# Gate products of a gated linear recurrence in three rounded parts instead of one full-precision product

## The chip, the cores and the metric

One core of one Trainium2 chip runs the whole program. The metric is the device time of one execution in microseconds (us). A core has a matrix engine (TensorE, PE in the profile; its weight loads are PEld), three elementwise engines (VectorE or DVE, ScalarE or ACT, GpSimd or POOL), and SyncE (SP), which issues the transfers from memory. Each engine works through its own instructions in order and waits on semaphores for the others.

## The reference, cut to what matters

Two transformer layers over 256 image tokens and 256 context tokens. Each layer mixes four branches; the third is a gated linear recurrence. Its input `u` is a convolution of four taps over a projection; two gates come from block-diagonal products with `u` (8 blocks of 128 channels), in two directions:

```python
def _rglru_gates(u, wa, ba, wx, bx, lam):
    B, L, C = u.shape
    ub = u.reshape(B, L, LRU_BLOCKS, LRU_BS)
    r = sigmoid(einsum('blnc,ncd->blnd', ub, wa).reshape(B, L, C) + ba)
    i = sigmoid(einsum('blnc,ncd->blnd', ub, wx).reshape(B, L, C) + bx)
    log_a = -LRU_C * softplus(-lam) * r
    a = exp(log_a)
    b = sqrt(-expm1(2.0 * log_a)) * (i * u)
    return a, b
...
    u = _dwconv(r_u, conv_c) + conv_c_b          # four taps
    uc = _dwconv(cr_u, conv_c) + conv_c_b
    rec_c, rec = _rglru_bidir(uc, u, lru_wa, lru_ba, lru_wx, lru_bx, lru_lam)
```

All arrays are float32.

## The kernel before, in words

Activations lie transposed, channels on the 128 partitions and the 512 tokens (256 image, 256 context) along the free axis, so that 1024 channels are 8 rows of 128 x 512. A large product is made of float32r parts: each operand is split into a rounded high part (names ending in H) and the rest (ending in L), and three products are summed, H with H, L with H and H with L. The weights stream through two slots of `RAW`, 1 MB slabs; ScalarE copies a slab to its high part `WH` in two halves, and GpSimd or VectorE subtracts it from `RAW` to get `WL`.

The change lies in the stage `c_in`, the first of each layer. For each of the 8 rows n it goes as follows.

- TensorE multiplies a slab: recurrence input (`ru`) and recurrence gate (`rg`) of row n, the function `ru_rg`. Then it makes the four gate products of row n - 1 (function `gates`, line 830): two directions by two gates, each 128 x 128 with 512 columns, here plain float32, straight from the convolved row in `TMP` and the gate weights in `CD`. A float32 product is two instructions in the trace.
- VectorE, in this order: `front` (bias and first tap, three further taps, first half of a gelu), `drives` and `scans` of row n - 2, `gelu`, `outputs` of row n - 2, `weights` of row n - 1 (the input gate times the convolved row, which needs the gate products), `lows` (the low parts of the slab after next, two halves), `sums` of row n - 1.
- ScalarE: `front` (copies `ru` out of PSUM), the square roots of row n - 2, `high` (the high parts of a slab), the tanh of `gelu`, `decays` of row n - 1 (eight activations from the gate products), `z_high`.
- GpSimd has no work in `c_in` beyond the low parts of the slab before it; its next slab is one of the stage `kv`.
- Before the first row of layer 0 VectorE works out the decay rates (`decay_rates`, line 1586), a chain of small instructions on the tile `LT`.

Layer 0 does all of it for 512 tokens; in layer 1 the gate half `rg` and what follows it is only needed for the 256 image tokens. After the last row comes a slab of the stage `kv`, then the gate products of row 7, the rest of `kv`, the stage `q` and the attention. The order on each engine is the order in which the code is written; nothing reorders it. The gate weights of a layer (2 MB) are loaded to `CD` before the layer; `ZH` and `ZL` hold the results of the branch from row 0 on, written by `z_high` and `z_out`.

Of the kernel before, what the change touches and what calls it, by code (L numbers as in the profile page):

```python
# [14 lines left out]
P = 128  # L15
# [9 lines left out]
KC = D // P  # L25
# [53 lines left out]

POOL_WHOLE = ("c_in", "kv", "q", "d_in", "c_out", "b_out", "a_cu", "a_b", "w_out")  # L80
WARM_UP = (2, 3)
GELU_C = 0.7978845608028654
# [86 lines left out]
def build(nc, stream, modw, lruw, xT, cT, prm, rope, consts, outT):  # L169
    with ExitStack() as ctx:  # L170
        def sb(name, n, dt=F32):
            return ctx.enter_context(nc.sbuf_tensor(name, [P, n], dt))

        def sem(name):
            return ctx.enter_context(nc.semaphore(name))
# [7 lines left out]
        G = sb("G", KC * GW)  # L183
        CD = sb("CD", KC * NT)
        PADA = sb("PADA", 2 * GW)
# [91 lines left out]
        def normed(nm):  # L277
            return (HH, HL) if nm == "n1" else (ZH, ZL)

        def lc(j, n, d):  # L280

            return LC[:, ds(n + (16 * j + 8 * d), 1)]
# [44 lines left out]
        def stage_sems(l):  # L327
# [3 lines left out]
            def st(name, names=""):  # L331
                a[name] = Steps(sem(f"{name}_{l}"), names)
# [22 lines left out]
            both("cf_a", "ru sq th", KC)  # L355
            st("cf_v", "u0 u1 u2 u3 p")
            st("ci_a", "r0 r1 i0 i1 t0 t1 a0 a1")
            st("ci_s", "s0 s1")
            st("ci_v", "iu0 iu1 w0 w1")
            st("ci_r", "b0 b1 h0 h1 rec y")  # L360
            st("ci_h", "zh")
# [148 lines left out]
        def _(pool):  # L510
# [7 lines left out]
            for s in range(2):  # L518
                for h in range(2):
                    low(0, s, h)  # L520
            runs = [(0, 1, 0)]
            for l in range(DEPTH):
# [20 lines left out]
            for first, end, halves in [r for r in runs if r[2]]:  # L543
                if first - 1 in ff_first:
                    first += 1
                for l in range(DEPTH):
                    if l > 0 and first == pair_base(l, "kv") + 1:
                        norm_low(l, "n1", 2)
                end_of = end - (end - 1 in ff_first)
                cuts = [pair_base(l, LAST_OUT) + x for l in range(DEPTH) for x in (0, 2)]  # L550
# [18 lines left out]
        def _(pe):  # L569
# [248 lines left out]
            for l in range(DEPTH):  # L818
# [11 lines left out]
                def gates(n):  # L830
                    pe.wait_ge(a["cf_v"].sem, a["cf_v"].at(n, "u3"))
                    if n > 0:
                        pe.wait_ge(a["ci_a"].sem, a["ci_a"].at(n - 1, "i1"))
                    for g in range(4):
                        last = mm(bank(4 + g), CD[:, n * NT + g * P:n * NT + (g + 1) * P], tmp(n % 2), True, True)
                    last.then_inc(a["ci_p"].sem, 1)

                pe.wait_ge(lru_loaded, 16 * (l + 1))
                if l > 0:
# [138 lines left out]
        def _(act):  # L978
# [163 lines left out]
            for l in range(DEPTH):  # L1142
# [30 lines left out]
                def gelu(n):  # L1173
                    s = n % 2
                    act.wait_ge(fv.sem, fv.at(n, "p"))
                    fn(seqs(tmp(4, 0, W), C), padded(n, C), ACT.Tanh, scale=GELU_C * GELU_A).then_inc(fa.sem, 1)

                def decays(n):
                    act.wait_ge(a["ci_p"].sem, n + 1)
# [17 lines left out]
                for n in range(KC):  # L1197
                    s, m = n % 2, b + n // 2
                    front(n)
                    if n > 1:  # L1200
                        roots(n - 2)
                    high(m + 1, s)
                    gelu(n)
                    if n > 0:
                        decays(n - 1)
                    if n > 1:
                        z_high(n - 2)
# [277 lines left out]
        def _(dve):  # L1485
# [141 lines left out]
            for l in range(DEPTH):  # L1627
# [150 lines left out]
                def gelu(n):  # L1778
                    s = n % 2
                    dve.wait_ge(fa.sem, fa.at(n, "th"))  # L1780
                    stt(padded(n, C), seqs(tmp(4, 0, W), C), 1.0, seqs(bank(2 * s + 1, W), C), ADD, MUL).then_inc(slab_out[s], 1)

                def weights(n):
                    for d in range(2):
# [40 lines left out]
                for n in range(KC):  # L1825
# [7 lines left out]
                    if n > 0:  # L1833
                        weights(n - 1)
                    lows(n + 2)
                    if n > 0:
# [568 lines left out]
```

## Time and profile before

| | |
|---|---|
| time, median of 3 | 1990.16 us (1989.03 to 1990.35) |
| span of the profiled execution | 1986.4 us |
| its mean granted TensorE clock | 0.997 |
| PE busy | 1962.3 us, 99% |
| DVE busy | 1369.2 us, 69% |
| ACT busy | 907.2 us, 46% |
| POOL busy | 810.8 us, 41% |
| chain that ended last | PE 90%, DVE 6%, ACT 3%, issue 1%, DMA 1% |
| stage `c_in`, first to last gate product | 56.3 to 158.9 us (layer 0), 1303.5 to 1389.8 us (layer 1) |

The profiled execution's own time is not listed apart from the three above; it has a span of 1986.4 us, and 3.8 us of the median lie outside of the span. Busy shares are means over stages with different limits. A matmul's end is modelled and overlaps the start of the next, so a matmul's cost is read from the distance of two starts. An instruction that waits for a port, and not for a semaphore, shows as a long one. In a timeline, a row merges instructions that follow each other on one line.

### The profile page before, as it was taken

The page shows a single profiled execution, that of the slowest core. Times are in us where ns is not written, and L with a number is a line of the kernel's source. Part 1 is how long each engine was busy: PE and PEld are TensorE (multiplying, and loading weights), DVE is VectorE, ACT ScalarE, POOL GpSimd, SP SyncE. Part 2 cuts the span into 40 slices and gives each one's busy share as a digit, 9 for nine tenths or more (in the row PEclk, how much of TensorE's full clock was granted, in tenths as well). Part 3 has the DMA queues.
Part 4 walks back from the last instruction along what each step waited for, and adds up shares of the span by engine and source line. Part 5 has one row for each costly group of instructions (what it writes and reads, how often), then busy time and mean ns, then how long its engine had stood idle before and what let it go on. Part 6 is the DMA issues. An engine that isn't in the chain of part 4 may idle for free.

```text
span 1986.4 us, 29293 instructions
## 1 busy us (share of the span) xinstructions
PE 1962.3 (99%) x11038; PEld 1665.0 (84%) x11038; DVE 1369.2 (69%) x2403; ACT 907.2 (46%) x1435; POOL 810.8 (41%) x353
## 2 busy tenths in 40 slices
PE   7999999999999999999999999999999999999998
PEld 5778888888888878878888888777999999999998
DVE  5896444567878868788885444589746888645555
ACT  5787544322222252245222222589955444565444
POOL 1002322343434444344344343400646887454442
PEclk9999999999999999999999999999999999999999
DMA  8222211222222234533554452312423555445453
GB/s 344 80 85 84 87 45 63 85 87 104 85 106 85 106 128 172 208 149 128 203 199 171 176 225 90 142 65 85 149 107 128 191 181 196 175 174 186 179 184 128
DMA packets 38701, 276.25 MB, mean 139 GB/s; under 512 B 4416, under 2 KB 4416, under 8 KB 6336
## 3 DMA queue, kind: packets, MB, share of 16 engines
q1 hardware_dynamic: 38592, 274.77, 37.3%
q8 instruction: 72, 1.18, 0.2%
q14 instruction: 37, 0.30, 0.0%
HBM read 273.70 MB, written 1.05 MB: 138 GB/s over the span
## 4 chain that ended last, share of the span: by engine, by line
PE 90%; DVE 6%; ACT 3%; issue 1%; DMA 1%; POOL 0%; SPq 0%; DVEq 0%; ACTq 0%; POOLq 0%
PE PS L571 89%; DVE PS L1492 1%; ACT WH L980 1%; PE PS L877 1%; DVE PS L1489 1%; ACT HH L980 0%; DVE HL L1492 0%; DVE ZL L1492 0%; DVE X L1492 0%; DMA RAW<-in_stream 0%; ACT PS L980 0%; ACT TMP L980 0%; DVE CD L1489 0%; PE PS L669 0%; DVE S L1492 0%
## 5 line engine op out<-in xcount | busy, mean ns | idle before, releaser
L514 POOL TENSOR_TENSOR WL<-RAW,WH 128x1024 fp32r<-128x1024 f32 (+1 forms) x337 | 801.7, 2397 | 1152.1 <-ACT WH L980 1152.0
L980 ACT ACTIVATE WH<-RAW 128x1024 fp32r<-128x1024 f32 (+1 forms) x416 | 414.7, 1043 | 622.9 <-PE PS L571 574.5
L571 PE MATMUL PS<-HH,WH 128*128 128x512 f32 (+2 forms) x1968 | 689.8, 351 | 4.0 <-issue 1.7
L571 PE MATMUL PS<-HH,WL 128*128 128x512 f32 (+2 forms) x1968 | 671.9, 342 | 0.0
L571 PE MATMUL PS<-HL,WH 128*128 128x512 f32 (+2 forms) x1968 | 669.4, 341 | 0.3 <-DVE HL L1492 0.2
L571 PE MATMUL PS<-ZH,WH 128*128 128x512 f32 (+1 forms) x1312 | 444.4, 339 | 3.4 <-DVE HL L1489 2.6
L571 PE MATMUL PS<-ZH,WL 128*128 128x512 f32 (+1 forms) x1312 | 443.8, 339 | 0.0
L571 PE MATMUL PS<-ZL,WH 128*128 128x512 f32 (+1 forms) x1312 | 441.7, 339 | 0.0
L571 PEld LDWEIGHTS PS<-HH,WH 128*128 128x128 f32 x1968 | 370.0, 188 | 58.5 <-issue 10.3
L571 PEld LDWEIGHTS PS<-HL,WH 128*128 128x128 f32 x1968 | 371.1, 189 | 51.7 <-issue 6.0
L571 PEld LDWEIGHTS PS<-HH,WL 128*128 128x128 f32 x1968 | 370.3, 188 | 45.9
L571 PEld LDWEIGHTS PS<-ZH,WH 128*128 128x128 f32 x1312 | 247.3, 188 | 34.5 <-issue 3.5
L571 PEld LDWEIGHTS PS<-ZH,WL 128*128 128x128 f32 x1312 | 247.4, 189 | 30.0
L571 PEld LDWEIGHTS PS<-ZL,WH 128*128 128x128 f32 x1312 | 246.8, 189 | 30.4 <-issue 0.4
L1492 DVE SCALAR_TENSOR_TENSOR PS<-G,PRM,PS 128x512 f32<-128x512 f32 (+1 forms) x464 | 254.3, 615 | 0.1
L980 ACT ACTIVATE TMP<-PS 128x512 f32<-128x512 f32 (+1 forms) x168 | 82.4, 490 | 99.2 <-PE PS L571 49.8
L1489 DVE TENSOR_TENSOR WL<-RAW,WH 128x1024 fp32r<-128x1024 f32 (+1 forms) x79 | 113.6, 1455 | 16.5 <-ACT WH L980 16.5
L1489 DVE TENSOR_TENSOR TMP<-TMP,PS 128x512 f32<-128x512 f32 (+1 forms) x54 | 30.4, 563 | 136.9 <-ACT TMP L980 122.7
L1489 DVE TENSOR_TENSOR PS<-TMP,PS 128x256 f32<-128x256 f32 (+1 forms) x82 | 45.0, 549 | 82.7 <-ACT TMP L980 71.7
L1492 DVE SCALAR_TENSOR_TENSOR PS<-CD,SILC,PS 128x512 f32<-128x512 f32 x112 | 84.7, 756 | 4.0
L1492 DVE SCALAR_TENSOR_TENSOR PS<-G,SILC,PS 128x512 f32<-128x512 f32 x112 | 84.7, 756 | 4.0
L1492 DVE SCALAR_TENSOR_TENSOR G<-G,PS 128x512 f32<-128x512 f32 (+1 forms) x16 | 8.9, 556 | 94.4 <-ACT G L980 94.4
(200 smaller groups left out, 1694.8 us busy)
## 6 DMA issues: line engine op xcount, KB each, us to landing
RAW<-in_stream SPq DMA_DIRECT2D x200, 1024.0 KB, 4.8
CD<-in_modw SPq DMA_DIRECT2D x22, 1024.0 KB, 7.0
G<-in_modw SPq DMA_DIRECT2D x22, 1024.0 KB, 7.2
RAW<-in_stream SPq DMA_DIRECT2D x8, 768.0 KB, 4.1
CD<-in_lruw SPq DMA_DIRECT2D x2, 2048.0 KB, 11.5
X<-in_xT SPq DMA_DIRECT2D x2, 1024.0 KB, 7.0
S<-in_modw SPq DMA_DIRECT2D x2, 1024.0 KB, 13.0
RAW<-in_modw SPq DMA_DIRECT2D x1, 1024.0 KB, 19.8
```

Of the source, the lines that this page charges most:

```text
L514: nc.gpsimd.tensor_tensor(WL[:, a:b], RAW[:, a:b], WH[:, a:b].bitcast(F32), ALU.subtract)\
L571: return nc.tensor.matmul(out, lhs, rhs, start=start, stop=stop)
L877: last = nc.tensor.transpose(bank(4 + u, P, q * P), PR[u % 2][:, q * P:(q + 1) * P], IDENT)
L980: return nc.scalar.activation(out, in_, f, **kw)
L1489: return V.tensor_tensor(out, x, y, op)
L1492: return V.scalar_tensor_tensor(out, x, sc, y, op0, op1)
```

## The change

The gate products become three float32r products each, like all others. VectorE and ScalarE split the convolved row for it: a new step on ScalarE, `driver_high`, copies it to its high part after the tanh of `gelu`, and a new step on VectorE, `driver_low`, subtracts, after `weights` and ahead of `lows`. Both parts lie in rows of `CD` from which the gate weights have been taken by then. GpSimd splits the gate weights once a layer, `CD` to `ZH` and `ZL`, a copy and a subtraction for each of the 8 rows in the order `GATE_ORDER`; the subtraction waits for its copy. TensorE waits for both. In layer 0 the steps stand behind GpSimd's first four subtractions, in layer 1 behind its six subtractions for the norm.

```diff
+GATE_ORDER = (0, 2, 3, 6, 7, 1, 4, 5)
...
+        def driver(n):
+            at = (2 + 4 * (n % 2)) * NT
+            return CDR[:, at:at + NT], CDR[:, at + NT:at + 2 * NT]
...
+            def gate_weights(l):
+                gh, gl = L[l]["gw_h"], L[l]["gw_l"]
+                pool.wait_ge(lru_loaded, 16 * (l + 1))
+                if l:
+                    read(pool, l - 1, LAST_OUT)
+                for j, n in enumerate(GATE_ORDER):
+                    nc.gpsimd.tensor_copy(row(ZH, n), row(CD, n)).then_inc(gh.sem, 1)
+                    pool.wait_ge(gh.sem, gh.at(j, "w"))
+                    nc.gpsimd.tensor_tensor(row(ZL, n), row(CD, n), row(ZH, n).bitcast(F32), ALU.subtract).then_inc(gl.sem, 1)
+            gate_weights(0)
...
                     if l > 0 and first == pair_base(l, "kv") + 1:
                         norm_low(l, "n1", 2)
+                        gate_weights(l)
...
                 def gates(n):
-                    pe.wait_ge(a["cf_v"].sem, a["cf_v"].at(n, "u3"))
+                    pe.wait_ge(a["cf_l"].sem, a["cf_l"].at(n, "u"))
+                    pe.wait_ge(a["gw_l"].sem, a["gw_l"].at(GATE_ORDER.index(n), "w"))
                     if n > 0:
                         pe.wait_ge(a["ci_a"].sem, a["ci_a"].at(n - 1, "i1"))
+                    uh, ul = driver(n)
                     for g in range(4):
-                        last = mm(bank(4 + g), CD[:, n * NT + g * P:n * NT + (g + 1) * P], tmp(n % 2), True, True)
+                        wh, wl = row(ZH, n, P, g * P), row(ZL, n, P, g * P)
+                        mm(bank(4 + g), wh, uh, True, False)
+                        mm(bank(4 + g), wh, ul, False, False)
+                        last = mm(bank(4 + g), wl, uh, False, True)
                     last.then_inc(a["ci_p"].sem, 1)
...
-                pe.wait_ge(lru_loaded, 16 * (l + 1))
...
+                def driver_high(n):
+                    act.wait_ge(fv.sem, fv.at(n, "u3"))
+                    if n > 1:
+                        act.wait_ge(a["ci_p"].sem, n - 1)
+                    else:
+                        act.wait_ge(a["gw_l"].sem, a["gw_l"].at(max(GATE_ORDER.index(x) for x in ((6, 7) if n else (2, 3))), "w"))
+                    fn(driver(n)[0], tmp(n % 2), ACT.Copy).then_inc(a["cf_h"].sem, 1)
...
                     gelu(n)
+                    driver_high(n)
                     if n > 0:
                         decays(n - 1)
...
+                def driver_low(n):
+                    uh, ul = a["cf_h"], a["cf_l"]
+                    dve.wait_ge(uh.sem, uh.at(n, "u"))
+                    high, rest = driver(n)
+                    tt(rest, tmp(n % 2), high.bitcast(F32), SUB).then_inc(ul.sem, 1)
...
                         weights(n - 1)
+                    driver_low(n)
                     lows(n + 2)
```

The rest of the diff gives the semaphores of these steps one counter for both layers and names the rounded view `CDR` of `CD`.

On GpSimd, at the start of the program, before: the low parts of the first two slabs, and then the loop of later stages.

```order
L514 ISA
L514 TENSOR_TENSOR WL<-RAW,WH 128x1024 [waits hi_done0] x2
L514 TENSOR_TENSOR WL<-RAW,WH 128x1024 [waits hi_done1] x2
L553 UNCONDITIONAL_BRANCH
L553 ISA
L514 TENSOR_TENSOR WL<-RAW,WH 128x1024 [waits hi_done0]
```

The same place now (`gw_h` is the copy's semaphore; a CAST is the copy to float32r):

```order
L529 TENSOR_TENSOR WL<-RAW,WH 128x1024 [waits hi_done0] x2
L529 TENSOR_TENSOR WL<-RAW,WH 128x1024 [waits hi_done1] x2
L543 CAST ZH<-CD 128x512 [waits lru_loaded]
L545 TENSOR_TENSOR ZL<-CD,ZH 128x512 [waits gw_h]
L543 CAST ZH<-CD 128x512
L545 TENSOR_TENSOR ZL<-CD,ZH 128x512 [waits gw_h]
L543 CAST ZH<-CD 128x512
```

Sixteen instructions stand now between the low parts of slab 1 and the loop.

On VectorE, in `c_in` of layer 0 from the gelu of row 3 on, before (`S<-S,TMP` is `weights`, `S<-S` behind `WL` is `sums`, the `TENSOR_SCALAR` is the first tap of row 4):

```order
L1492 SCALAR_TENSOR_TENSOR G<-TMP,PS 128x2x256 [waits cf_a]
L1489 TENSOR_TENSOR CD<-TMP 128x512 [waits ci_r_0]
L1492 SCALAR_TENSOR_TENSOR TMP<-CD,G 128x512 [waits slab_out1,ci_r_0]
L1492 SCALAR_TENSOR_TENSOR S<-S,TMP 128x512 [waits ci_a_0] x2
L1489 TENSOR_TENSOR WL<-RAW,WH 128x1024 [waits hi_done1] x2
L1492 SCALAR_TENSOR_TENSOR S<-S 128x512 [waits ci_v_0,ci_a_0] x2
L1495 TENSOR_SCALAR TMP<-G,PRM 128x512 [waits cf_a,ci_v_0,ci_p_0]
```

The same place now:

```order
L1533 SCALAR_TENSOR_TENSOR G<-TMP,PS 128x2x256 [waits cf_a]
L1530 TENSOR_TENSOR CD<-TMP 128x512 [waits ci_r]
L1533 SCALAR_TENSOR_TENSOR TMP<-CD,G 128x512 [waits slab_out1,ci_r]
L1533 SCALAR_TENSOR_TENSOR S<-S,TMP 128x512 [waits ci_a] x2
L1530 TENSOR_TENSOR CDR<-TMP,CDR 128x512 [waits cf_h]
L1530 TENSOR_TENSOR WL<-RAW,WH 128x1024 [waits hi_done1] x2
L1533 SCALAR_TENSOR_TENSOR S<-S 128x512 [waits ci_v,ci_a] x2
L1536 TENSOR_SCALAR TMP<-G,PRM 128x512 [waits cf_a,ci_v,ci_p_0]
```

One instruction is new, `CDR<-TMP,CDR`, behind `weights` and ahead of `WL`. TensorE's gate products wait for it.

## Rows read from the trace of the kernel before

**Rows 1.** Timeline of TensorE, layer 0: start us, us, engine line op tiles.
```profile
56.34 3.59 PE L571 MATMUL PS<-TMP,CD 128*128 128x512 f32 x8
60.00 0.40 PE L571 MATMUL PS<-HL,WH 128*128 128x512 f32 x1
60.24 0.40 PE L571 MATMUL PS<-HH,WL 128*128 128x512 f32 x1
```

**Rows 2.** The same view: gate products of row 7 (layer 0), rows 4, 6, 7 (layer 1).
```profile
158.87 1.45 PE L571 MATMUL PS<-TMP,CD 128*128 128x512 f32 x3
...
1351.23 1.02 PE L571 MATMUL PS<-TMP,CD 128*128 128x512 f32 x2
...
1375.09 0.59 PE L571 MATMUL PS<-TMP,CD 128*128 128x512 f32 x1
...
1389.82 2.74 PE L571 MATMUL PS<-TMP,CD 128*128 128x512 f32 x6
```

**Rows 3.** Windows: us, PE, PEld, DVE, ACT, POOL busy (x), PEclk, DMA.
```profile
114.08:128.62 14.54, 14.54 (x57) 10.38 (x56) 14.03 (x21) 12.98 (x18) 0.00 (x0) 1.00 0.20 73
...
1341.31:1354.03 12.72, 12.72 (x59) 9.24 (x58) 12.58 (x20) 12.66 (x19) 0.00 (x0) 1.00 0.24 82
...
1280.00:1285.00 5.00, 4.72 (x22) 3.86 (x20) 2.30 (x6) 4.82 (x10) 2.68 (x2) 0.78 0.01 2
```

**Rows 4.** Timeline of ScalarE and VectorE: a copy and a subtraction of 128x512.
```profile
83.18 0.63 ACT L980 ACTIVATE ZH<-S 128x512 fp32r<-128x512 f32 x1
...
85.28 0.68 DVE L1489 TENSOR_TENSOR ZL<-S,ZH 128x512 fp32r<-128x512 f32 x1
85.88 2.31 DVE L1492 SCALAR_TENSOR_TENSOR TMP<-G,PRM,TMP 128x512 f32<-128x512 f32 x3
```

**Rows 5.** Timeline of VectorE: first taps of rows 0, 2; lows behind weights.
```profile
49.76 0.55 DVE L1495 TENSOR_SCALAR TMP<-G,PRM 128x512 f32<-128x512 f32 x1
...
67.70 0.55 DVE L1495 TENSOR_SCALAR TMP<-G,PRM 128x512 f32<-128x512 f32 x1
...
81.34 2.35 DVE L1489 TENSOR_TENSOR WL<-RAW,WH 128x1024 fp32r<-128x1024 f32 x2
...
1313.72 0.54 DVE L1495 TENSOR_SCALAR TMP<-G,PRM 128x512 f32<-128x512 f32 x1
...
1350.56 2.35 DVE L1489 TENSOR_TENSOR WL<-RAW,WH 128x1024 fp32r<-128x1024 f32 x2
```

**Rows 6.** Timeline of GpSimd and VectorE side by side, two places.
```profile
42.70 4.73 POOL L514 TENSOR_TENSOR WL<-RAW,WH 128x1024 fp32r<-128x1024 f32 x2 [19.25 <-ACT WH L980]
42.81 4.66 DVE L1489 TENSOR_TENSOR LT<-LT 128x16 f32<-128x16 f32 x2
...
47.71 1.64 DVE L1492 SCALAR_TENSOR_TENSOR LT<-LT 128x16 f32<-128x16 f32 x8
...
189.25 5.22 POOL L514 TENSOR_TENSOR WL<-RAW,WH 128x1024 fp32r<-128x1024 f32 x2 [8.04 <-ACT WH L980]
...
190.32 4.71 DVE L1489 TENSOR_TENSOR PS<-TMP,CD 128x512 f32<-128x512 f32 x2
```

**Rows 7.** Instructions on tile ZL: duration ns min/median/max, first and last start us.
```profile
L1492 DVE SCALAR_TENSOR_TENSOR ZL<-S,MOD,ZH x6: 473/829/2081, 909.9 to 921.6; 128x256 fp32r<-128x256 f32 x6
```

**Rows 8.** GpSimd by form: count, busy us, mean ns, idle before and its releasers.
```profile
L514 POOL TENSOR_TENSOR WL<-RAW,WH 128x1024 fp32r<-128x1024 f32 x325 | 779.7, 2417 | 1114.1 <-ACT WH L980 1114.1
...
L538 POOL TENSOR_TENSOR HL<-S,HH 128x256 fp32r<-128x256 f32 x6 | 4.4, 739 | 3.0 <-ACT S L980 3.0
```

**Rows 9.** Timeline of SyncE and GpSimd; and DMA issues, median us to landing.
```profile
25.03 0.33 SPq L471 DMA_DIRECT2D CD<-in_lruw  x1
...
1293.72 0.73 POOL L538 TENSOR_TENSOR HL<-S,HH 128x256 fp32r<-128x256 f32 x1 [0.57 <-ACT S L980]
...
CD<-in_lruw SPq DMA_DIRECT2D x1, 2048.0 KB, 14.0
```

**Rows 10.** TensorE's waits from 1240 to 1560: total us, times, longest.
```profile
PE PS L877 <- DVE PADA L1495: 0.6, 1, 0.6
```

More of the change, by code:

```diff
@@ L172, in sb, with sb_and_rounded @@
             return ctx.enter_context(nc.sbuf_tensor(name, [P, n], dt))
+        def sb_and_rounded(name, n):
+            at = (nc.sbuf_base + 31) // 32 * 32
+            return sb(name, n), nc.alloc_sbuf_tensor_at(name + "R", [P, n], F32R, offset=at)
         def sem(name):
@@ L183, in build @@
         G = sb("G", KC * GW)
-        CD = sb("CD", KC * NT)
+        CD, CDR = sb_and_rounded("CD", KC * NT)
         PADA = sb("PADA", 2 * GW)
@@ L355, in stage_sems @@
             both("cf_a", "ru sq th", KC)
[L356 to L360, printed above, removed]
+            both("cf_v", "u0 u1 u2 u3 p", KC)
+            both("ci_a", "r0 r1 i0 i1 t0 t1 a0 a1", KC)
+            both("ci_s", "s0 s1", KC)
+            both("ci_v", "iu0 iu1 w0 w1", KC)
+            both("ci_r", "b0 b1 h0 h1 rec y", KC)
+            both("gw_h", "w", KC)
+            both("gw_l", "w", KC)
+            both("cf_h", "u", KC)
+            both("cf_l", "u", KC)
             st("ci_h", "zh")
```

## The prediction

> **What bounds the kernel now.** I read the timeline of TensorE first. In `c_in` of layer 0 the gate products of row 0 start at 56.34 us [rows 1] and those of row 7 at 158.87 [rows 2]: seven rows of 14.65 us. In layer 1 rows 4 and 6 are 23.86 us apart, 11.93 a row [rows 2]. Then the windows of one row: TensorE is busy for all of it in both layers, GpSimd not at all, VectorE for 14.03 of 14.54 us in layer 0 and for 12.58 of 12.72 in layer 1 [rows 3]. The reader is to see that "TensorE bounds" is only half true here. A row of layer 1 takes VectorE 12.72 us and TensorE 11.93: VectorE falls behind by 0.8 us a row, and TensorE doesn't notice, since its gate products only wait for the convolution, early in VectorE's row. Last I read GpSimd and VectorE side by side. A subtraction of 128x16 that takes VectorE about 0.17 us takes 4.66 us for two while GpSimd makes two slab halves in 4.73, ending with them [rows 6].
>
> **The gate products.** Before, eight instructions from 56.34 to one slot of 0.24 ahead of 60.00, that is to 59.76: 3.42 us, 0.43 each. After, twelve at the 0.24 (0.232 to 0.235) of an ordinary product [rows 1]: 2.78 us. That is 0.65 us a row, 10.4 us for 16 rows, if TensorE waits for nothing.
>
> **VectorE.** One subtraction of 128x512 more a row: 0.68 us long, 0.60 from start to start [rows 4]. Layer 0: 14.03 busy plus small gaps make about 14.1, with it 14.7 us a row, against TensorE's new 14.65 - 0.65 = 14.0. Layer 1: 12.72 + 0.60 = 13.33 against 11.93 - 0.65 = 11.28. VectorE is now the slower in both, and the gate products wait for it: `driver_low` stands behind `weights`, 9.2 us into VectorE's row (1341.31 [rows 3] to 1350.56 [rows 5]), and not behind the third tap, 3 us into it. Its slack in the old times, layer 1, row 4: `weights` ends at 1350.56 [rows 5], with the subtraction at 1351.2, and the gate products started at 1351.23 [rows 2]: none. Queued behind it are `lows`, `sums` and the next `front`.
>
> **ScalarE.** One copy of 0.63 us a row, 0.53 from start to start [rows 4]. In layer 1 it is busy for 12.66 of 12.72 us [rows 3], but much of that is that it follows VectorE; 12.8 us with the copy stay under 13.33. Cost nothing while VectorE is slower. It also moves `decays` back by 0.53 us, hidden likewise.
>
> **Without GpSimd** the sum would be this. Layer 0: at row 2 `driver_low` would end at 81.34 + 0.6 [rows 5], 3.7 us ahead of the gate products at 56.34 + 2 x 14.65 = 85.6; that slack shrinks by 0.7 us a row and just lasts, so TensorE keeps 0.65 a row for 7 of 8 rows; `c_in` ends 4.6 us earlier. Layer 1: row 2 is reached at 1375.09 - 4 x 11.93 - 2 x 0.65 = 1326.1; from there the gate products follow VectorE, row 6 comes at 1326.1 + 4 x 13.36 = 1379.5, and row 7 a `kv` slab later: 1389.82 - 1375.09 - 3.42 = 11.3 [rows 2], plus 2.78: 1393.6, which is 3.8 us late. The two nearly cancel.
>
> **GpSimd.** A subtraction took it 2.42 us at 1024 columns, 0.74 at 256 [rows 8], so 1.29 at 512. A copy to float32r isn't in the trace. From below: ScalarE's 0.63 [rows 4]; from above: the subtraction's 1.29, which reads two operands. I take 0.9, near the middle. 16 instructions are then about 17.5 us in each layer. The start is when GpSimd is free: 47.4 us in layer 0 [rows 6] (the weights landed at 25.03 + 14.0 = 39.0), and 1294.5 in layer 1 [rows 9], in both just as `c_in` begins.
>
> What it costs is the port. [rows 6] show the pattern: a VectorE instruction with two operands in SBUF, issued inside a GpSimd instruction, ends just after it (two in 4.66 beside two in 4.73; 4.71 for two 0.7 us ones at 190.32), and GpSimd waits for it in turn (5.22 for the two at 189.25). It holds for SCALAR_TENSOR_TENSOR too: 0.473 us at least, 2.08 at most [rows 7]. So the two take turns. Nearly all of `c_in` on VectorE has two such operands: decay rates, three taps, `weights`, `driver_low`, `lows`, `sums`.
>
> The Trainium skill says this as a rule (SBUF — State Buffer, Who interferes with whom): the shared port pair is an exclusive lock held for the whole instruction, and two SBUF inputs on VectorE contend with any GpSimd instruction that reads SBUF. By that the copies hold it as well as the subtractions, which no row shows. The sum below agrees with the rule. Its GPSIMD Engine Reference (Elementwise side by side) gives a one-operand loop of 512 elements 0.77 us; with that for my 0.9 the sum would be about 17 us in place of 19.
>
> *Layer 0.* The eight dependent instructions on `LT` took 1.64 us [rows 6]; now each waits for one GpSimd instruction: 4 x (0.9 + 1.29) = 8.8 from 47.4, plus 1.0 for their own turns: 57.2. Row 0's first tap moves from 49.76 [rows 5] to 57.6. Three taps wait in turn, 3 us more; gelu at 65.0, `driver_low` done and gate products at 66.5, **10.2 us late**; TensorE has nothing else to do, as `gates(0)` stands ahead of slab 2 in its queue. `lows` and two GpSimd turns: 70.8, row 1 by 79.2, TensorE at 66.5 + 14.0 = 80.5. Row 2's first tap at 82.6; from it to the end of `weights` took 81.34 - 67.70 = 13.6 [rows 5], of which some 3 were idle, plus `driver_low`: 93.5, TensorE again 94.5. Then VectorE's 14.7 a row from 93.5: rows 3 to 7 at 108.2, 122.9, 137.6, 152.3, 167.0. Row 7 at 167.0 against 158.87, less 0.65: **+7.5 us**. Behind it layer 0 has no TensorE wait, and I take it that VectorE's own shift of 8 us stays hidden behind TensorE's 7.5.
>
> *Layer 1.* Row 0's taps each wait: its gelu ends 2.3 late, `driver_high(0)` needs the third split row (1303.2), gate products at 1304.7. `lows` waits twice, row 1's taps three times, `weights` once or twice: row 1 at 1320.8 (5.4 late), row 2's first tap at 1324.2 for 1313.72 [rows 5]. GpSimd ends at 1319.5. Row 2 at 1334.0, then 13.36 a row: row 6 at 1387.5, row 7 after the `kv` slab, + 14.1: 1401.5, for 1389.82: **+11.7 us**. Here nothing is given back: the attention starts on VectorE's chain already (TensorE waited 0.6 us for it) [rows 10], and that chain moves by VectorE's 11.7.
>
> Sum: 7.5 + 11.7 = 19.2 us on a span of 1986.4; with the 3.8 outside of it, 2009.4 for the median of 1990.16. With a copy of 0.65 it is 14.7, with 1.29 it is 24; if copies don't hold the port, 9.9.
>
> The clock: over 1280 to 1285 us, where TensorE has gaps (4.72 busy of 5), the mean granted was 0.78: 2.2 us at 1.2 GHz and not 2.4, a loss of 1.1 [rows 3]. A TensorE idle for 10 us in layer 0 may bring the like. It would be lost ahead of row 4, where VectorE takes over anyway, and costs next to nothing.
>
> **The rivals.** (1) *The port doesn't bite*: the two engines' instructions slip past each other, as these are half as long as the slab halves or less, and the subtraction in VectorE's row is all that is left to set against the shorter products. For it: no row shows this pair of shapes. Against: [rows 6], at the very tile in question. Then only the row lengths count: -4.6 + 3.8, 1989.4, no change. (2) *TensorE keeps its pace*, for VectorE's row has reserves that I don't see, and the products are all that matters: -10.4, 1979.8. For it: TensorE waits almost nowhere before. Against: the slack of none at row 4 of layer 1. (3) *Only subtractions hold the port*: +9.9, 2000. Rivals 1 and 2 are the side that is not slower. What decides is the place of `gates(0)` in layer 0: on time in both, 2 us late in rival 3, 10 us late in the forecast. The forecast turns into "slower" as soon as the two layers' last gate products come over 5 us late together.
>
> **How the numbers follow.** Forecast 0.78, with 2003 to 2015 as its own range (copy of 0.65 to 1.29, and a GpSimd semaphore wait of 0 to 0.3 us in each of eight pairs); rival 3 0.10; rival 1 0.06; rival 2 0.06. A difference under 0.2% (4 us) can't be told from none. Faster 0.06, same 0.06, slower 0.88. The range, 1997 to 2016, leaves out rivals 1 and 2 and a little of the forecast's upper end. Predicted: 2009.
>
> **What would show it.** Right: a TensorE wait of about 10 us for `CDR` ahead of the first gate products in layer 0; the eight instructions on `LT` at about 1.2 us each; in layer 1 a wait ahead of nearly every row's gate products, rows 13.3 us apart, VectorE without idle; gate products of row 7 at about 167 and 1401; twelve products in 2.8 us. Wrong: `LT` instructions at 0.17 us while GpSimd copies (then the copy holds nothing, rival 3), rows of layer 1 at 11.3 us (rival 2), or a GpSimd copy far from 0.9 us, which shifts each layer by about 2 us per 0.2.

## The result, and the profile after

The changed kernel takes 2004.9 us (median of 4 runs, 2001.8 to 2006.4) against 1989.9 for the kernel before beside it: a ratio of 1.0069, 95% interval 1.0057 to 1.0082, some 14 us slower. The forecast was 2009 in a range of 1997 to 2016. The profiled execution has a span of 2003.1 us, 16.7 more than before, at a granted clock of 0.992 for 0.997. In nearly every execution on record with both numbers the time is 1.7 to 1.8 us above the span (2004.86 for 2003.1 here), not the 3.8 that was put down for the kernel before. By that, its profiled execution took about 1988.2 us (an estimate), some 2 us under its median, and the 16.7 is too large by as much.

GpSimd and VectorE at the start of `c_in` in layer 0, in the timeline of the changed kernel (start us, us, engine, line, operation, tiles). They answer to [rows 5, 6].

```profile
45.56 2.41 POOL L529 TENSOR_TENSOR WL<-RAW,WH 128x1024 fp32r<-128x1024 f32 x1
47.91 0.62 POOL L543 CAST ZH<-CD 128x512 fp32r<-128x512 f32 x1
48.60 1.31 POOL L545 TENSOR_TENSOR ZL<-CD,ZH 128x512 fp32r<-128x512 f32 x1
...
48.80 5.60 DVE L1533 SCALAR_TENSOR_TENSOR LT<-LT 128x16 f32<-128x16 f32 x8
54.43 1.35 DVE L1536 TENSOR_SCALAR LC<-LT 128x16 f32<-128x16 f32 x2
...
55.91 0.72 DVE L1536 TENSOR_SCALAR TMP<-G,PRM 128x512 f32<-128x512 f32 x1
...
56.66 4.33 DVE L1533 SCALAR_TENSOR_TENSOR TMP<-G,PRM,TMP 128x512 f32<-128x512 f32 x3
...
63.02 0.90 DVE L1530 TENSOR_TENSOR CDR<-TMP,CDR 128x512 fp32r<-128x512 f32 x1
63.83 3.44 DVE L1530 TENSOR_TENSOR WL<-RAW,WH 128x1024 fp32r<-128x1024 f32 x2
67.20 0.54 DVE L1536 TENSOR_SCALAR TMP<-G,PRM 128x512 f32<-128x512 f32 x1
67.77 2.33 DVE L1533 SCALAR_TENSOR_TENSOR TMP<-G,PRM,TMP 128x512 f32<-128x512 f32 x3
```

The eight instructions on `LT` took 1.64 us before and take 5.60 here, the three taps 4.33 for 2.33. Behind GpSimd's last instruction they are at 2.33 again (row 1, 67.77). The first tap has moved from 49.76 to 55.91.

GpSimd's instructions by form, in `c_in` of layer 0 (40 to 70 us) and of layer 1 (1290 to 1330): count, busy us, mean ns, idle time before. They answer to [rows 8].

```profile
L545 POOL TENSOR_TENSOR ZL<-CD,ZH 128x512 fp32r<-128x512 f32 x8 | 11.0, 1381 | 0.6
L543 POOL CAST ZH<-CD 128x512 fp32r<-128x512 f32 x8 | 5.8, 729 | 0.0
...
L545 POOL TENSOR_TENSOR ZL<-CD,ZH 128x512 fp32r<-128x512 f32 x8 | 12.2, 1531 | 0.6
L543 POOL CAST ZH<-CD 128x512 fp32r<-128x512 f32 x8 | 7.9, 991 | 0.0
```

A copy on its own is 0.61 or 0.62 us, a subtraction 1.31; the means hold GpSimd's own turns of waiting.

Gate products of rows 0 and 7 in layer 0, rows 3, 4 and 7 in layer 1, from TensorE's timeline, with what it waited for in brackets. They answer to [rows 1, 2].

```profile
63.97 1.22 PE L599 MATMUL PS<-CDR,ZH 128*128 128x512 f32 x2 [6.74 <-DVE CDR L1530]
...
164.57 0.73 PE L599 MATMUL PS<-CDR,ZH 128*128 128x512 f32 x2
...
1350.84 0.86 PE L599 MATMUL PS<-CDR,ZH 128*128 128x512 f32 x2 [1.88 <-DVE CDR L1530]
...
1364.17 0.73 PE L599 MATMUL PS<-CDR,ZH 128*128 128x512 f32 x2 [0.23 <-DVE CDR L1530]
...
1404.81 0.62 PE L599 MATMUL PS<-CDR,ZH 128*128 128x512 f32 x2
```

Windows of one row of layer 0, of two rows of layer 1, and of the first gate products: length, then busy us of PE, PEld, DVE, ACT, POOL, and the granted clock. They answer to [rows 3].

```profile
122.23:136.33 14.10, 14.10 (x62) 11.27 (x60) 13.96 (x21) 13.50 (x19) 0.00 (x0) 1.00 0.20 74
1337.52:1350.84 13.32, 11.44 (x60) 9.67 (x61) 13.18 (x21) 13.26 (x21) 0.00 (x0) 1.00 0.22 79
1350.84:1364.17 13.33, 13.10 (x61) 10.79 (x61) 13.19 (x21) 13.27 (x22) 0.00 (x0) 0.87 0.22 80
...
61.00:68.00 7.00, 4.03 (x10) 3.21 (x11) 6.24 (x7) 4.01 (x6) 3.90 (x4) 0.51 0.00 0
```

In layer 0 TensorE is busy through the row; in layer 1 it has 1.9 us of a row to spare, and VectorE sets the 13.32. After some of the waits in layer 1 the granted clock falls: the row from 1350.84, which began after a wait of 1.88 us, has 0.87 and leaves TensorE 0.2 us to spare. That costs nothing, as VectorE's row is as long as before. `c_in` of layer 0 ends 5.1 us late (164.57 against 158.87, less the 0.65 by which the twelve products are shorter). Layer 1's first slab product starts at 1290.50 for 1284.23, 6.3 late. Its last gate products start 15.0 late, less 0.65: 14.3. So layer 1 adds 8.0 us, and 1.2 came between the layers. The change has no work there; a fall of the granted clock, which comes in some executions and not in others, accounts for it. Here is a stretch between the layers in the changed kernel, the same place in the kernel before, and that place in before_rates_early (an experiment below):

```profile
945.00:949.00 4.00, 4.00 (x12) 3.08 (x12) 3.82 (x6) 0.54 (x2) 3.92 (x2) 0.57 0.00 0
...
941.00:949.00 8.00, 8.00 (x36) 6.44 (x35) 6.96 (x11) 0.60 (x1) 2.89 (x2) 1.00 0.26 81
...
941.00:945.00 4.00, 4.00 (x11) 3.10 (x11) 3.82 (x6) 1.32 (x2) 4.00 (x2) 0.57 0.00 0
```

The granted clock was 0.57 for these 4 us in the changed kernel and 1.00 in the kernel before; but it was 0.57 too in before_rates_early, which has none of the change, and 8 of the 14 profiles on record have the like there. The rest, 2.4 of 16.7, came behind `c_in` of layer 1 in small steps; other kernels' profiles drift by up to 3 us there too, and no run here isolates it.

### The profile page after: what moved, and what is told of

Same layout as the page of the kernel before. It is cut to its first block, busy times and chain, and to the rows that moved or that the text cites. A ratio compares the mean times of both kernels' runs of the same rounds, so it can differ in the third digit from the quotient of the medians.

```text
span 2003.1 us, 29504 instructions
## 1 busy us (share of the span) xinstructions
PE 1966.2 (98%) x11102; PEld 1685.9 (84%) x11102; DVE 1392.2 (70%) x2419; ACT 914.5 (46%) x1451; POOL 850.2 (42%) x385
## 4 chain that ended last, share of the span: by engine, by line
PE 80%; DVE 9%; ACT 4%; DMA 2%; POOL 2%; issue 2%; SPq 0%; DVEq 0%; POOLq 0%; ACTq 0%
PE PS L599 79%; POOL WL L529 2%; DVE PS L1533 1%; DVE TMP L1533 1%; DMA RAW<-in_stream 1%; ACT WH L1012 1%; DMA CD<-in_modw 1%; PE PS L909 1%; DVE WL L1530 1%; ACT HH L1012 1%; DVE S L1533 1%; ACT S L1012 0%; DVE ZL L1533 0%; DVE HL L1533 0%; ACT TMP L1012 0%
```

## The experiments

All against the kernel before on the same chip. Where the interval holds 1, the run can't be told from the kernel before; differences of 0.2% with an interval clear of 1 are told from it, but only just.

| run | median us | before | ratio, 95% interval |
|---|---|---|---|
| split_only | 2000.3 | 1990.4 | 1.0055 (1.0041 to 1.0069) |
| driver_only | 1995.0 | 1990.4 | 1.0025 (1.0015 to 1.0034) |
| no_split | 1990.8 | 1990.4 | 1.0002 (0.9993 to 1.0012) |
| products_only | 1986.4 | 1990.4 | 0.9981 (0.9972 to 0.9990) |
| rates_early | 2002.9 | 1990.2 | 1.0064 (1.0051 to 1.0077) |
| driver_early | 2004.8 | 1990.2 | 1.0066 (1.0050 to 1.0082) |
| layer0_tuned | 1989.5 | 1990.2 | 0.9997 (0.9989 to 1.0006) |
| before_rates_early | 1990.3 | 1990.2 | 0.9998 (0.9989 to 1.0007) |
| copies_24 | 1993.7 | 1990.6 | 1.0018 (1.0008 to 1.0027) |
| subtractions_8 | 1994.0 | 1990.6 | 1.0017 (1.0008 to 1.0026) |
| fills_24 | 1990.3 | 1990.6 | 0.9995 (0.9986 to 1.0004) |
| layer0_six_rows | 1986.9 | 1990.6 | 0.9979 (0.9971 to 0.9988) |

### The change taken apart

**split_only**, against the changed kernel:

```diff
-                        wh, wl = row(ZH, n, P, g * P), row(ZL, n, P, g * P)
-                        mm(bank(4 + g), wh, uh, True, False)
...
+                        last = mm(bank(4 + g), CD[:, n * NT + g * P:n * NT + (g + 1) * P], tmp(n % 2), True, True)
...
-                    driver_high(n)
...
-                    driver_low(n)
```

> The kernel before with one part of the change alone: GpSimd splits the gate weights into ZH and ZL at the start of each `c_in` (16 instructions a layer), and nothing reads what it makes; the gate products stay eight in float32, VectorE's row has no new subtraction and ScalarE's no new copy. What is computed is that of the kernel before. Theory (port): the 16 GpSimd instructions make VectorE's two-operand instructions wait their turn, and that alone is the largest term. With the durations now seen in the changed kernel (0.61 us the copy, 1.3 the subtraction) the first gate products of layer 0 start at about 61.7 us for 56.34 and those of row 7 stay 5.6 us late; in layer 1 VectorE's row of 12.7 us is moved by about 4 us. Sum: +10 us, some 2000. The eight instructions on LT take over 5 us together and not 1.64. Rival A (dependence): GpSimd itself costs nothing, what made the changed kernel slower is that the gate products wait for a copy, a subtraction and the split weights: then this kernel is at 1990, within 1 us of the kernel before. Rival B (longer row of VectorE only): likewise 1990.

Measured: 9.9 us slower in the medians, as the port theory has it. ScalarE got two new waits for the end of the split here, so that `ZH` isn't overwritten too early; in the trace it never stood for GpSimd. Instructions whose result nobody reads cost two thirds of the whole change, so rivals A and B fall. VectorE's timeline:

```profile
45.99 6.77 DVE L1531 SCALAR_TENSOR_TENSOR LT<-LT 128x16 f32<-128x16 f32 x8
52.80 1.37 DVE L1534 TENSOR_SCALAR LC<-LT 128x16 f32<-128x16 f32 x2
...
55.03 4.38 DVE L1531 SCALAR_TENSOR_TENSOR TMP<-G,PRM,TMP 128x512 f32<-128x512 f32 x3
```

The profiled execution was the fastest of its five (1995.7; the others 1999.4 to 2002.4), with the first gate products at 59.47 and not 61.7 and those of row 7 3.3 us late: there the chain on `LT` had started beside the slab halves already (45.99, and 48.80 in the changed kernel's profile) and met GpSimd's new instructions less. That the spread of the five comes from where the two engines meet is likely, not shown.

**driver_only**, which keeps the lines on the driver, moves its two parts to rows 6 and 7 of `ZH` and `ZL`, and drops `gate_weights` and the three products:

```diff
-            at = (2 + 4 * (n % 2)) * NT
-            return CDR[:, at:at + NT], CDR[:, at + NT:at + 2 * NT]
+            at = (6 + n % 2) * NT
+            return ZH[:, at:at + NT], ZL[:, at:at + NT]
...
-            gate_weights(0)
```

> The second part alone: ScalarE's copy and VectorE's subtraction make the high and the low part of the convolved row (in rows 6 and 7 of ZH and ZL), and the gate products wait for the low part but stay eight in float32 on the unsplit row; GpSimd splits nothing. Theory (VectorE's row): layer 0 has 14.7 us a row on TensorE and 14.7 on VectorE, so nothing is lost there; in layer 1 VectorE's row grows from 12.7 to 13.33 us over TensorE's 11.93, TensorE is caught from row 3 or 4, and the last gate products come about 4.5 us late. Sum: +4.5 us, 1994 to 1995. Rival A (dependence): the wait for copy and subtraction costs in both layers, from row 0 on: about 1 us at row 0 of each layer and kept, +2 on top. Rival C (the port alone): VectorE's added subtraction is covered, within 1 us of the kernel before.

Measured: 4.6 us slower. TensorE's timeline, row 7 of layer 0 and rows 4 to 6 of layer 1:

```profile
159.32 3.60 PE L597 MATMUL PS<-TMP,CD 128*128 128x512 f32 x8
...
1355.02 3.70 PE L597 MATMUL PS<-TMP,CD 128*128 128x512 f32 x8 [1.13 <-DVE ZL L1522]
1368.34 3.70 PE L597 MATMUL PS<-TMP,CD 128*128 128x512 f32 x8 [1.12 <-DVE ZL L1522]
1381.67 3.70 PE L597 MATMUL PS<-TMP,CD 128*128 128x512 f32 x8 [1.25 <-DVE ZL L1522]
```

Layer 0 lost nothing (159.32, after a front that was 0.5 late); layer 1 runs at 13.33 us a row and waits for the subtraction each time. Rivals A and C fall.

**no_split**: as driver_only, but with twelve products.

```diff
-                        wh, wl = row(ZH, n, P, g * P), row(ZL, n, P, g * P)
+                        wh, wl = uh[:, g * P:(g + 1) * P], ul[:, g * P:(g + 1) * P]
```

> Twelve products a row and the split of the convolved row as in the changed kernel, but GpSimd splits nothing: in place of the gate weights each product takes 128 columns of the row's high or low part as its weights, so the gates are other numbers. Theory (port): with GpSimd's part gone, TensorE gains 0.65 us a row in layer 0 (row 7 at about 155.0 for 158.87, the stage 4.6 us earlier) and loses 3 to 4 us in layer 1, where rows 3 to 7 follow VectorE at 13.33 us. Sum: -1.5 us (-1 to 0), 1988.5 to 1990. The changed kernel is then slower than this one by 14 to 16 us, all of it GpSimd's. Rival A (dependence on copy and subtraction): nearly as slow as the changed kernel, +10 or more. Rival D (the granted clock: twelve short products in place of eight long ones lower it): slower than the kernel before by over 2 us, with half-clock stretches in both layers.

Measured: no difference (0.4 us, interval -1.4 to 2.4), just above what was expected; the changed kernel is slower than this one by some 13 us. What differs is GpSimd's split, with the waits for it; split_only says that its instructions alone make up most of that. TensorE's timeline, the first gate product of rows 6 and 7 of layer 0 and of row 5 of layer 1:

```profile
140.39 0.50 PE L597 MATMUL PS<-ZH 128*128 128x512 f32 x1 [0.51 <-DVE ZL L1526]
...
155.05 0.50 PE L597 MATMUL PS<-ZH 128*128 128x512 f32 x1 [0.51 <-DVE ZL L1526]
...
1363.11 0.50 PE L597 MATMUL PS<-ZH 128*128 128x512 f32 x1 [1.91 <-DVE ZL L1526]
```

Row 7 of layer 0 comes 3.8 us early, at 155.05 for the 155.0 expected, with VectorE's row of 14.66 us just catching TensorE (waits of 0.51 at rows 6 and 7); and layer 1 gives it back. Rival D falls: layer 0 has no stretch at half clock, layer 1 has one of 3.4 us at 1338, and the time is not longer.

**products_only**: as no_split, but `driver_low` is gone too, and the high part serves for all three; the products wait for ScalarE's copy. Against no_split:

```diff
-                    pe.wait_ge(a["cf_l"].sem, a["cf_l"].at(n, "u"))
+                    pe.wait_ge(a["cf_h"].sem, a["cf_h"].at(n, "u"))
...
-                        wh, wl = uh[:, g * P:(g + 1) * P], ul[:, g * P:(g + 1) * P]
+                        wh, wl = uh[:, g * P:(g + 1) * P], uh[:, g * P:(g + 1) * P]
...
-                        mm(bank(4 + g), wh, ul, False, False)
+                        mm(bank(4 + g), wh, uh, False, False)
...
-                    driver_low(n)
```

> As the run without GpSimd's split, and VectorE's subtraction is gone as well: ScalarE's copy makes the high part, which the twelve products of a row use three times over, for weights too, so the gates are other numbers. What is left of the change is twelve products of 2.78 us for eight of 3.42, and the copy. Theory: layer 0 gains 0.65 us for each row, 5.3 us; in layer 1 VectorE's row stays 12.7 us, longer than TensorE's 11.28, and eats the gain from row 4 on: the last gate products come 1 us late or on time. Sum: -4 us, about 1986. Rival 2 of the prediction (TensorE keeps its pace): -10.4 us, 1979.8.

Measured: 4.1 us faster, and not 10.4. The saving in the products is real in layer 0 and worth little in layer 1, where VectorE's old row of 12.7 us is already longer than TensorE's. ScalarE, with its copy, is as full there (12.74 us busy of a row of 12.80, VectorE 12.66), so this run doesn't say which of the two holds the row.

### What in GpSimd's split costs

**rates_early**: `decay_rates(0)` moved to where VectorE waits for the sum of squares.

```diff
+                    decay_rates(0)
                     dve.wait_ge(a["n1_a"].sem, KC + 1)
...
-                    decay_rates(0)
```

> The changed kernel with one thing moved: VectorE computes layer 0's decay rates (the chain of instructions on LT) before the first norm, where it waits anyway, and not at the start of `c_in`. Theory (port, on the path through LT): the chain no longer stands ahead of row 0's first tap, so GpSimd's copies and subtractions only meet row 0's taps: first gate products at about 58 us for 63.97, row 7 at 159.6 for 164.57, layer 0 within 0.5 us of the kernel before and not 4.8 behind. Layer 1 is untouched. Sum: about 4.5 to 5 us under the changed kernel, 2000. Rival A (what delays layer 0 is the wait for the split weights of row 0 or for the copy and subtraction): no gain, 2005. Rival E (the LT chain is only replaced by longer taps, since GpSimd works for 17 us either way): a gain of 1 to 2 us.

Measured: in the trace layer 0 comes as expected. VectorE, ScalarE's copy of row 0, and TensorE (rows 0 and 7):

```profile
45.94 5.49 DVE L1533 SCALAR_TENSOR_TENSOR TMP<-G,PRM,TMP 128x512 f32<-128x512 f32 x3
...
55.30 0.64 ACT L1012 ACTIVATE CDR<-TMP 128x512 fp32r<-128x512 f32 x1 [2.48 <-POOL ZL L545]
...
57.74 0.73 PE L599 MATMUL PS<-CDR,ZH 128*128 128x512 f32 x2 [0.50 <-DVE CDR L1530]
...
159.76 0.73 PE L599 MATMUL PS<-CDR,ZH 128*128 128x512 f32 x2 [0.51 <-DVE CDR L1530]
```

Row 7 starts 4.8 us earlier than in the changed kernel, though the taps now meet GpSimd for longer (5.49), and though ScalarE's copy now stands 2.48 us for the third split row, which frees its place in `CD`. In the medians only 2 of these show (12.8 us over the kernel before, for 15.0), with intervals that overlap; the profiled execution was the fastest of its five, 3.1 us under their median. The sum is not settled by this run, only the place. Rival A, who expected no gain, falls for layer 0.

**driver_early**: copy and subtraction earlier in their rows.

```diff
                     high(m + 1, s)
+                    driver_high(n)
                     gelu(n)
-                    driver_high(n)
...
+                    driver_low(n)
                     gelu(n)
...
-                    driver_low(n)
```

> The changed kernel with another thing moved: ScalarE's copy of the convolved row stands ahead of the tanh, and VectorE's subtraction right behind the scans, so TensorE's gate products can start some 3 us earlier in VectorE's row. Theory: in layer 0 the late start stays (GpSimd), but from it TensorE's own 14.0 us a row rule: row 7 about 2.4 us earlier; in layer 1 VectorE's row of 13.33 us is the bound however its instructions are ordered, so the end comes only 0.8 us earlier. Sum: 3 us under the changed kernel, 2001 to 2002. Rival A (the place of the subtraction in the row is what makes TensorE wait, so moving it undoes most): under 1996.

Measured: no gain (14.6 us over the kernel before). Row 7 starts at 163.16 and 1402.08, 1.4 and 2.7 us earlier than in the changed kernel, yet the span is 2003.6. Layer 1's gain was lost at once: of its lead over the changed kernel 0.9 us was left at the first product of the attention (1443.09 for 1444.03) and none at 1450, with waits of 1.8 us for GpSimd's slab halves (1.0 in the changed kernel) and 1.36 for VectorE, whose chain had not become shorter. In layer 0 TensorE paid for a granted clock of 0.50 behind its wait: row 0 to row 1 took 16.5 us, the rows behind it 13.9 each. My expectation was 3 us too good; rival A, who wanted under 1996, is far off.

**before_rates_early**, the control: the same move in the kernel before.

> The control: the kernel before with the decay rates before the first norm and nothing else. Theory: TensorE bounds all of layer 0's `c_in`, so the 4.66 us that two instructions of the chain waited there for GpSimd were worth nothing: 0, within 1 us of the kernel before. Rival G (the chain was on the path in the kernel before too): faster by 2 us or more, and the gain of the two runs beside it would have to be read against that.

Measured: 0.2 us. The 4.66 us that the chain waited in [rows 6] cost nothing before; the same chain is on the path once GpSimd works on behind the slab.

**copies_24, subtractions_8, fills_24**: split_only with another loop body on GpSimd.

copies_24, where each copy waits for the one before it:

```diff
                     nc.gpsimd.tensor_copy(row(ZH, n), row(CD, n)).then_inc(gh.sem, 1)
                     pool.wait_ge(gh.sem, gh.at(j, "w"))
-                    nc.gpsimd.tensor_tensor(row(ZL, n), row(CD, n), row(ZH, n).bitcast(F32), ALU.subtract).then_inc(gl.sem, 1)
+                    nc.gpsimd.tensor_copy(row(ZH, n), row(CD, n)).then_inc(ch.sem, 1)
+                    pool.wait_ge(ch.sem, ch.at(j, "u"))
+                    nc.gpsimd.tensor_copy(row(ZH, n), row(CD, n)).then_inc(gl.sem, 1)
```

fills_24 has `nc.gpsimd.memset(row(ZH, n).bitcast(F32), 0.0)` in place of each of the three copies. subtractions_8 has one instruction a row and no wait:

```diff
-                    nc.gpsimd.tensor_copy(row(ZH, n), row(CD, n)).then_inc(gh.sem, 1)
-                    pool.wait_ge(gh.sem, gh.at(j, "w"))
-                    nc.gpsimd.tensor_tensor(row(ZL, n), row(CD, n), row(ZH, n).bitcast(F32), ALU.subtract).then_inc(gl.sem, 1)
+                    nc.gpsimd.tensor_tensor(row(ZL, n), row(CD, n), row(CD, n), ALU.subtract).then_inc(gl.sem, 1)
```

> The kernel before with 24 GpSimd copies of 128x512 to float32r at the start of each `c_in` (each row of the gate weights copied three times over, one after the other) and no subtraction; nothing reads them. It asks whether a copy holds the port. Theory (a copy holds it as a subtraction does): some 16 us of GpSimd work; each of VectorE's two-operand instructions waits for the end of one copy, 0.6 us at most: first gate products of layer 0 at about 58.3, layer 0 +2.2 us, layer 1 +4: about +6, 1996. Rival 3 of the prediction (only subtractions hold it): 0, 1990.

> The kernel before with 8 GpSimd subtractions of 128x512 at the start of each `c_in` (each row of the gate weights less itself) and no copy; nothing reads them. 10.4 us of GpSimd work and not 16. Theory (what counts is how long the one instruction is that each VectorE instruction waits behind, and how many such turns fall into the LT chain, not GpSimd's busy time): layer 0 +5.6, layer 1 +2.4, together +8 us, 1998: more than 24 copies cost, for two thirds of the busy time. Rival H (the price goes with GpSimd's busy time): two thirds of what the 24 copies cost, 4 us or less.

> As with 24 copies, but each is a GpSimd memset of the same 128x512 row, which writes SBUF and reads nothing. Theory (any GpSimd instruction on SBUF holds the port): the LT instructions and the taps wait for each one's end as for a copy; if one takes 0.6 us as a copy does, +6 us, 1996, and if it takes 0.3 us, +1 or less. Rival I (only what reads SBUF holds the port): 0, with VectorE's instructions at their free durations in the middle of memsets.

Measured: +3.1, +3.5 and -0.2 us. VectorE's instructions on `LT` and its three taps, first with the copies:

```profile
48.68 3.18 DVE L1534 SCALAR_TENSOR_TENSOR LT<-LT 128x16 f32<-128x16 f32 x8
...
53.38 3.01 DVE L1534 SCALAR_TENSOR_TENSOR TMP<-G,PRM,TMP 128x512 f32<-128x512 f32 x3
```

with the subtractions:

```profile
49.57 6.37 DVE L1529 SCALAR_TENSOR_TENSOR LT<-LT 128x16 f32<-128x16 f32 x8
```

and with the memsets, with the GpSimd instruction at their side:

```profile
52.24 0.53 POOL L546 MEMSET ZH<- 128x512 f32 x1
...
50.62 1.64 DVE L1534 SCALAR_TENSOR_TENSOR LT<-LT 128x16 f32<-128x16 f32 x8
52.30 0.52 DVE L1537 TENSOR_SCALAR LC<-LT 128x16 f32<-128x16 f32 x2
...
53.67 2.33 DVE L1534 SCALAR_TENSOR_TENSOR TMP<-G,PRM,TMP 128x512 f32<-128x512 f32 x3
58.03 2.35 DVE L1531 TENSOR_TENSOR WL<-RAW,WH 128x1024 fp32r<-128x1024 f32 x2
```

So a copy holds VectorE off as a subtraction does, which rival 3 of the prediction denied; a memset of as many bytes does not hold off these instructions, since `LT`, taps and `WL` are at their free 1.64, 2.33 and 2.35 us: rival I is right on them and on the time, and my theory for the memsets wrong (the exception, TENSOR_SCALAR, stands in the last section). The sizes were too large for the other two. The subtraction of a row from itself took 1.06 us and not 1.3, and each turn came out shorter. By the medians 24 copies and 8 subtractions cost the same, so neither the length theory (+8) nor rival H is confirmed by them; the trace has the length theory's mark, 3.18 against 6.37 us for the same eight instructions. In the two profiled executions row 7 of layer 0 starts at 161.95 with the subtractions and at 159.29 with the copies, for 158.87 before: in layer 0 the copies cost next to nothing, so what they cost in the medians comes behind it.

### Towards a faster kernel

**layer0_tuned**: both moves above, split and three products in layer 0 only.

```diff
+                    if l == 0:
                         pe.wait_ge(a["cf_l"].sem, a["cf_l"].at(n, "u"))
...
+                        else:
+                            last = mm(bank(4 + g), CD[:, n * NT + g * P:n * NT + (g + 1) * P], tmp(n % 2), True, True)
...
-                        gate_weights(l)
```

> A version meant to beat both: three products and the split in layer 0 only, where TensorE bounds; layer 1 as in the kernel before; decay rates before the first norm, copy and subtraction early in their rows as in the two runs beside it. Theory: in layer 0 gate products start at about 57.8 us and run at TensorE's 14.0 us a row to 142 us (row 6), row 7 at 156.7; `c_in` ends 2.8 us earlier than before; layer 1 adds nothing. Sum: -2.8 us, 1987.5 on the 1990.4 of the kernel before. Rival F (the time gained in layer 0 is given back later, for another queue is late by then): 1990.

Measured: no difference (-0.6 us). The gate products came as foreseen, at 57.23 and 156.50; what I had left out stands right behind them. TensorE and VectorE:

```profile
156.50 0.62 PE L598 MATMUL PS<-CDR,ZH 128*128 128x512 f32 x2
...
161.13 0.35 PE L598 MATMUL PS<-WH,HH 128*128 128x256 f32 x1 [1.69 <-issue]
...
158.67 2.35 DVE L1537 TENSOR_TENSOR WL<-RAW,WH 128x1024 fp32r<-128x1024 f32 x2
```

TensorE stands for 1.69 us before the next `kv` slab, until VectorE's `lows` end at 161.02. The trace names no releaser ("issue"), the end of `WL` does. VectorE's row of 14.66 us had caught up, and that slab paid.

**layer0_six_rows**: rows 6 and 7 keep the float32 products, and the driver's parts lie in the free rows 6 and 7 of `ZH` and `ZL`.

```diff
+SPLIT = 6
+GATE_ORDER = (0, 1, 2, 3, 4, 5)
...
-                    if l == 0:
+                    if l == 0 and n < SPLIT:
```

> The tuned layer 0 again, now with three products for rows 0 to 5 only: rows 6 and 7 keep eight products in float32, so GpSimd splits six rows, and VectorE and ScalarE have nothing added in the last two rows; the high and low part of the convolved row lie in rows 6 and 7 of ZH and ZL, so row 0 waits for no other row's split. Layer 1 as in the kernel before. Theory (in the tuned version VectorE's row of 14.7 us caught TensorE at row 5, and the subtractions of the `kv` slab came 1.6 us late): first gate products at 56.4, six rows at 14.0, VectorE on time for the `kv` slab, `c_in` ends 3.5 us earlier than before. Sum: -3.5 us, 1986.7. Rival F (gained in layer 0, given back later): within 1 us of the kernel before.

Measured: 3.7 us faster in the medians, ratio 0.9979 (0.9971 to 0.9988), which is faster than both kernels. The first products came at 57.25 and row 7 at 154.86, 4.0 us early:

```profile
57.25 0.39 PE L599 MATMUL PS<-ZH 128*128 128x512 f32 x1
...
140.13 3.59 PE L599 MATMUL PS<-TMP,CD 128*128 128x512 f32 x8
...
154.86 3.60 PE L599 MATMUL PS<-TMP,CD 128*128 128x512 f32 x8
```

With no work for VectorE added in the last two rows, that `kv` slab is on time, and the medians show the gain. The profiled execution doesn't: its span is 1986.4 us, that of the kernel before. It was the second slowest of its twelve (1988.15), had a stretch of granted clock 0.58 from 936 that the profile of the kernel before lacks, and that profile was a fast execution.

## Why the prediction was right

**Gate products, as said.** Twelve take 2.8 to 2.9 us (164.57 to 167.47), and their worth alone is 4 us, not 10.4 (products_only).

**VectorE's row, as said.** 14.66 us in layer 0 (`driver_low` at 149.17 and 163.83) and 13.32 in layer 1. "Without GpSimd" was to be -4.6 and +3.8, nearly nothing: no_split is at 0.4.

**GpSimd and the port, as said.** The mechanism, its place in the `LT` chain, and both layers are there; split_only is the largest part. The parts add up within their noise: 10.9 (split_only) + 5.0 (driver_only) - 4.6 (no_split less driver_only) = 11.3 by the ratios, against 13.7 (11.3 to 16.3) for the whole.

**Mis-sized: the copy.** Taken at 0.9 us between 0.63 and 1.29, it is 0.61 to 0.62, the lower bound: ScalarE's copy was the near row, not the two-operand subtraction. Four turns on `LT` at 0.3 less make 1.2; GpSimd was through at 65.05, before row 1's taps. The taps lost 2.0 us and not 3. So the first products come at 63.97 and not 66.5, row 7 at 164.57 and not 167.0: 5.1 us for 7.5. In layer 1 the prediction did not take off the 0.65; counted like that, it has 8.7 for 11.7, and the two layers have 13.8 for 19.2. There GpSimd was through at 1321.1, less the shift of 6.3 that is 1314.8, and not at 1319.5, and row 2 comes at 1337.52, less the shift 1331.2, and not at 1334.0.

**Mis-sized, and hidden by luck: the turns on `LT`.** The prediction let each of the eight instructions wait for one GpSimd instruction, about 1.2 us each; they took 0.70 each. By its count, with the durations measured, the chain would have taken 4 x (0.61 + 1.31) + 1.0 = 8.7 us, and it took 5.60. Two terms that it had at nothing gave back 2.5 of these 3.1: the chain on `LT` ahead of the eight met GpSimd too, so that they started at 48.80 and not 47.4, and the instructions between them and the first tap took 1.5 us and not 0.4. So the first tap, at 55.91 for 57.6, came out nearer than its parts. That the sum of 14.7 "with a copy of 0.65" fits the measured 13.7 (by the ratio) to 15.0 (in the medians) rests partly on this.

**The clock, as said in its effect.** The window 61 to 68 us has 0.51: TensorE stood for 6.7 us, then made row 0's products at 1.2 GHz, 0.43 us apart for most of them and not 0.235, some 1.9 us longer. Little of that reached the end of the layer, since row 7's products start at 164.57, the moment VectorE's subtraction ends (163.83 + 0.69). But not nothing: ScalarE waited for TensorE's late slab of row 2, and VectorE then for ScalarE, so up to 0.8 us of it may be in VectorE's chain (an estimate from these rows of the changed kernel; no run isolates it):

```profile
80.13 0.60 ACT L1012 ACTIVATE TMP<-PS 128x512 f32<-128x512 f32 x1 [2.52 <-PE PS L599]
...
87.07 0.69 DVE L1533 SCALAR_TENSOR_TENSOR G<-TMP,PS 128x512 f32<-128x512 f32 x1 [0.82 <-ACT TMP L1012]
```

In driver_early, where TensorE paces the rows, all of it counted. The prediction had no clock term for layer 1, where the granted clock fell as well (0.87 in a row above), at no cost.

**Too simple:** in the prediction VectorE's row sets the pace of layer 0 from row 2 on. TensorE paced rows 1 to 6 at 14.10 us, and VectorE, at 14.66, reached it just at row 7.

## What to carry to other kernels

Before work goes to an idle GpSimd, count the VectorE instructions with two operands in SBUF (the on-chip memory) beside it: each waits for the end of the GpSimd instruction it meets, so a chain of tiny ones pays most, and it pays on the path even if its waits cost nothing before. The one-operand TENSOR_SCALARs waited likewise (the two on `LC` took 1.35 us for 0.25, the first tap 0.72 for 0.55), while the gelu step `G<-TMP,PS`, with one operand in PSUM, took its free 0.69 at 61.03, beside a GpSimd copy. Move such chains out of the way, and give new work to the stage in which the other engine is the bound and only for as many rows as VectorE has slack. A shorter engine A is worth nothing where B's row is already longer: read the row length of both, and the first slab behind the loop as well.

## What was not expected of the hardware

- GpSimd's memset of 128x512 (0.53 us) leaves VectorE's two-operand instructions alone, but not its TENSOR_SCALAR: the two on `LC`, 0.25 us together when free (in subtractions_8), took 0.52 from 52.30 on and ended just after the memset that ran from 52.24 to 52.77 (rows above); the first tap took 0.75 for 0.55 there. This is from one execution.
- Small VectorE instructions slip in where GpSimd stops: between a copy's end (48.53) and the subtraction's start (48.60) one on `LT` took 0.18 us, and the one behind it 1.15, to the subtraction's end; the next then waited 0.52 for the copy. So the chain made three steps for each copy with its subtraction, and not two. subtractions_8, whose instructions have no wait between them and leave no gap, allowed one step for each (0.96 to 0.97 us) while they lasted.
- GpSimd's subtraction of a tile from itself took 1.06 us, that of two tiles 1.31.
